# The high half of the weights stored as two areas of 16-column runs, read alternately by TensorE

## The reference: what is computed

```python
proj = h @ w_in[l]                       # 1024 x 7584, split into the branches
y_mla = mla_branch(...)                  # @ w_uq, @ w_ukv, @ w_o
y_conv = conv_branch(...)                # @ w_pw
y_ret = retention_branch(...)            # @ w_o
merged = gates[:, :, 0] * y_mla + gates[:, :, 1] * y_conv + gates[:, :, 2] * y_ret
x = x + rms_norm_2(merged @ w_out[l], ln_mix_post[l])
h = rms_norm_2(x, ln_ffn_pre[l])
f = (jax.nn.silu(h @ ffn_w_gate[l]) * (h @ ffn_w_up[l])) @ ffn_w_down[l]
x = x + rms_norm_2(f, ln_ffn_post[l])
```

## Time and profile before

| | |
|---|---|
| median of 3 runs | 1239.05 us |
| lowest, highest | 1238.3, 1243.12 us |
| span of the profiled execution, first to last instruction | 1235.8 us |
| what the median has beyond that span | 3.25 us |
| TensorE (PE) busy | 1205.2 us, 98% |
| VectorE (DVE) busy | 901.5 us, 73% |
| ScalarE (ACT) busy | 639.1 us, 52% |
| mean DMA rate | 175 GB/s |
| mean granted TensorE clock | 0.995 of 2.4 GHz |

### The profile page before, as it was taken

One profiled execution on the slowest core, in us unless ns is written; L12 is line 12 of the kernel. 1 busy time (PEld: TensorE's weight loads), 2 busy tenths in 40 slices (PEclk: granted clock), 3 DMA queues, 4 the chain that ended last, 5 costly groups with the idle time before them and its releaser, 6 DMA issues.

```text
span 1235.8 us, 19035 instructions
## 1 busy us (share of the span) xinstructions
PE 1205.2 (98%) x7597; PEld 1013.5 (82%) x7597; DVE 901.5 (73%) x1463; ACT 639.1 (52%) x1034; POOL 100.4 (8%) x163
## 2 busy tenths in 40 slices
PE   7999999999999999999999999999999999999998
PEld 3566778888988788787999987988788787999986
DVE  7998877757589998687666655589997687665553
ACT  4334565665556665545444544556575545444441
POOL 6300011101000200201000001000200201000000
PEclk9999999999999999999999999999999999999999
DMA  7635666434565555354766664565445355565552
GB/s 251 221 94 173 205 208 191 156 119 146 163 205 168 155 157 187 133 169 164 216 201 188 193 195 154 174 211 169 158 153 188 132 170 170 190 197 193 191 194 75
DMA packets 71958, 215.68 MB, mean 175 GB/s; under 512 B 16256, under 2 KB 19744, under 8 KB 71744
## 3 DMA queue, kind: packets, MB, share of 16 engines
q1 hardware_dynamic: 65008, 206.37, 52.0%
q0 software_dynamic: 2112, 6.97, 1.8%
q10 hardware_dynamic: 4752, 1.14, 0.4%
HBM read 208.95 MB, written 3.15 MB: 172 GB/s over the span
## 4 chain that ended last, share of the span: by engine, by line
PE 86%; DVE 8%; ACT 3%; issue 2%; POOL 1%; DMA 0%; DVEq 0%; POOLq 0%; ACTq 0%
PE acc L700 17%; PE acc L702 17%; PE acc L701 17%; PE acc L678 7%; PE acc L680 7%; PE acc L679 7%; PE acc L639 3%; PE mixed L1015 1%; DVE weights_lo L1776 1%; PE mixed L1112 1%; ACT junk L1279 1%; PE turned L755 1%; DVE h_T L1806 1%; PE mixed L999 1%; PE mixed L1008 1%
## 5 line engine op out<-in xcount | busy, mean ns | idle before, releaser
L1776 DVE TENSOR_TENSOR weights_lo<-weights_raw,weights_hi 128x1024 fp32r<-128x1024 f32 (+1 forms) x304 | 355.7, 1204 | 71.6 <-ACT weights_hi L1244 71.0
L1244 ACT ACTIVATE weights_hi<-weights_raw 128x1024 fp32r<-128x1024 f32 (+1 forms) x304 | 305.8, 1043 | 80.8 <-DMA weights_raw<-stream_dram 80.6
L700 PE MATMUL acc<-weights_hi,act_F_hi 128*128 128x512 f32 (+1 forms) x680 | 275.7, 406 | 5.6 <-DVE act_F_lo L1806 3.4
L702 PE MATMUL acc<-weights_hi,act_F_lo 128*128 128x512 f32 (+1 forms) x680 | 267.2, 393 | 0.0
L701 PE MATMUL acc<-weights_lo,act_F_hi 128*128 128x512 f32 (+1 forms) x680 | 265.4, 390 | 0.0
L678 PE MATMUL acc<-act_F_hi,weights_hi 128*128 128x256 f32 x624 | 173.6, 278 | 0.0
L679 PE MATMUL acc<-act_F_hi,weights_lo 128*128 128x256 f32 x624 | 172.5, 276 | 0.0
L680 PE MATMUL acc<-act_F_lo,weights_hi 128*128 128x256 f32 x624 | 172.4, 276 | 0.0
L700 PEld LDWEIGHTS acc<-weights_hi,act_F_hi 128*128 128x128 f32 x680 | 128.7, 189 | 34.2 <-DVE act_F_lo L1806 4.3
L702 PEld LDWEIGHTS acc<-weights_hi,act_F_lo 128*128 128x128 f32 x680 | 128.4, 189 | 28.4
L701 PEld LDWEIGHTS acc<-weights_lo,act_F_hi 128*128 128x128 f32 x680 | 128.7, 189 | 25.6
(11 more groups left out here) (339 smaller groups left out, 1923.6 us busy)
## 6 DMA issues: line engine op xcount, KB each, us to landing
weights_raw<-stream_dram SPq DMA_DIRECT2D x306, 512.0 KB, 3.7
weights_raw_more<-stream_dram SPq DMA_DIRECT2D x58, 512.0 KB, 4.3
gains<-rows_dram POOLq DMA_DIRECT2D x12, 512.0 KB, 4.8
weights_raw<-stream_dram SPq DMA_DIRECT2D x6, 416.0 KB, 3.1
weights_raw<-stream_dram SPq DMA_DIRECT2D x4, 384.0 KB, 3.5
x_T<-x_in_dram SPq DMA_DIRECT2D x4, 256.0 KB, 6.0
ssm_bc<-ssm_bc_dram SPq DMA_DIRECT2D x1, 1024.0 KB, 8.6
u_scratch<-u_T ACTq DMA_DIRECT2D x4, 256.0 KB, 5.5
```

The costliest lines, as they stand in the source:

```text
L700: pe.matmul(o, xh, wh, start=first and kk == 0, stop=False)
L702: i = pe.matmul(o, xl, wh, start=False, stop=last and kk == s["nk"] - 1)
L1244: act.activation(high(s, slice(0, n)), whole(s, slice(0, n)), ACT.Copy).then_inc(hi_made, 1)
L1776: dve.tensor_tensor(low(s, slice(0, n)), whole(s, slice(0, n)), high(s, slice(0, n)).bitcast(F32), ALU.subtract).then_inc(lo_made, 1)
```

## The change

In every slot that goes the rows-held way, the high half is stored in another order. The 1024 columns are taken as runs of 16 columns (64 bytes); the even runs go to the first half of the place, the odd runs to the second half, 2048 bytes further on. For the moving operand, TensorE gets an access pattern with three dimensions (16 pairs of runs, 2 areas, 16 columns), so that it takes a run from one area and a run from the other in turn. The columns reach the array in the old order, and the results are written to PSUM contiguously, as before. ScalarE writes the high half through the new pattern and VectorE reads it back through it; the raw weights and the low half keep their order. Slots that go the channels-held way are unchanged. No instruction is added, removed or moved on any engine, and no tile changes its address.

```diff
+LINE = 16
...
+        def channels_held(s):
+            name = slots[s]["chunk"]
+            return name in with_channels and not name.endswith(".ffn.0")
+
+        def halves_apart(s, x):
+            if channels_held(s):
+                return x
+            return x.rearrange("p (h i c) -> p i h c", h=2, c=LINE)
+
+        def lines_in_order(s, x):
+            if channels_held(s):
+                return x
+            return x.rearrange("p (i h c) -> p i h c", h=2, c=LINE)
+
+        def in_halves(s, kk):
+            n = slots[s]["nk"] * slots[s]["width"]
+            x = high(s, slice(0, n)).rearrange("p (h k i c) -> p k i h c", h=2, k=slots[s]["nk"], c=LINE)
+            return x[:, kk]
...
@@ tile_slot (rows held)
-                    wh, wl = (f(at, slice(kk * w, (kk + 1) * w)) for f in (high, low))
+                    wh, wl = in_halves(at, kk), low(at, slice(kk * w, (kk + 1) * w))
...
@@ make_hi, on ScalarE
-                act.activation(high(s, slice(0, n)), whole(s, slice(0, n)), ACT.Copy).then_inc(hi_made, 1)
+                act.activation(halves_apart(s, high(s, slice(0, n))), lines_in_order(s, whole(s, slice(0, n))), ACT.Copy).then_inc(hi_made, 1)
...
@@ make_lo, on VectorE
-                dve.tensor_tensor(low(s, slice(0, n)), whole(s, slice(0, n)), high(s, slice(0, n)).bitcast(F32),
-                                  ALU.subtract).then_inc(lo_made, 1)
+                dve.tensor_tensor(lines_in_order(s, low(s, slice(0, n))), lines_in_order(s, whole(s, slice(0, n))),
+                                  halves_apart(s, high(s, slice(0, n)).bitcast(F32)), ALU.subtract).then_inc(lo_made, 1)
```

## The result

The changed kernel takes **1257.47 us**, median of four runs (1255.34 to 1261.55), against 1238.67 us for the kernel before (four runs, 1235.68 to 1243.12). The ratio is 1.0158, 95% interval 1.0129 to 1.0187: **slower by 1.6%**, 18.8 us. The profiled execution took 1255.34 us with a span of 1253.5 us, 17.7 us more than the span before; the mean granted clock is 0.996 (0.995 before), so the clock plays no part.

The account below looks back on a forecast made before the run. TensorE was taken to set the pace, through the distance between matmuls. Span 1235.8 less 11.9 us from the high-half stream, other steps at nothing, gave 1223.9; plus 3.25 for the median, 1227 us, range 1213 to 1264.

Parts of the forecast that it names:

- The place: Effect expected in L700 and L702, 2030 matmuls streaming the high half; L701 and channels-held matmuls untouched.
- the two bounds: Rows-held high-half matmul: from 12.9 ns less (23.6 us gained) to 13.3 ns more (24.3 us lost).
- half of the excess: High-half stream: 16 of some 31 cycles beyond a clean stream saved per matmul, 6.5 ns, 11.9 us less.
- Rival 2: L700 and L702: each change of area costs one more TensorE cycle, 13.3 ns, 24.3 us slower, 1263; chance 0.28.
- Rival 1: Moving stream: fetch rate limits it whatever the order of 64-byte runs; no change, 1239 within 5; chance 0.30.
- Rival 3: High-half stream: all 12.9 ns come back, 23.6 us, 1215; upper part of the faster case, whose chance is 0.42.
- The term 1.83 us per ns: High-half matmuls: one nanosecond on each of 2030 is 2.03 us of streaming, 1.83 us of it on the chain.
- the share of 0.90: Rows-held lines: 630 us of their 697 us of streaming taken to lie on the chain that sets the end.
- The steps costed at nothing: ScalarE's write and VectorE's read in two areas: no cost taken; bad end 66 and 76 ns per slot, about 1 us.
- a faster TensorE that meets VectorE: Near 435 and 885 us VectorE has 2% left; a rows-held stream 2% shorter was said to just fit.
- The range: Whole kernel: from the clean stream, 1213, to one full cycle per run, 1264, leaving out only a larger loss.
- The chances: Whole kernel: faster 0.42, no change 0.30, slower 0.28.

Follow-up runs that it names:

- the fifth run: TensorE-only program, not the kernel: 512-column matmuls streaming every fifth 16-column piece, 320 bytes apart; 228.7 ns each, as contiguous.
- the runs of 64: The changed kernel with pieces of 64 columns in place of 16, slots of 416 columns contiguous; 1238.12 us, ratio 1.0002 to the kernel before.
- the areas at 2112 bytes: Kernel before, but TensorE alternates 16-column pieces from areas 2112 bytes apart, 128 bytes on in each, in 512-column slots; 1237.2 us, ratio 0.9998.
- the last row of the table: TensorE-only program: 16-column pieces from two areas 2048 bytes apart, 128 bytes on in each; 233.3 ns per matmul, one group.
- the stores alone: The changed kernel with TensorE reading the high half contiguously, ScalarE and VectorE keeping the two-area pattern; 1238.28 us, ratio 0.9999 to the kernel before.
- the first small program: No kernel: TensorE alone runs 24 matmuls for each of 28 access patterns; contiguous 228.7 ns, the change's pattern 240.0 ns.
- TensorE's pattern alone: The changed kernel with ScalarE's and VectorE's steps contiguous again, TensorE still reading two areas; 1261.91 us, ratio 1.0191 to the kernel before.
- runs of 32: The changed kernel with pieces of 32 columns in place of 16, slots not divisible by 64 contiguous; 1247.51 us, ratio 1.0081 to the kernel before.
- the last kernel: The kernel before with activation operands that only rows-held products read moved to the weights' address modulo 256 bytes; 1235.18 us, ratio 0.9981.

## Why the prediction was wrong

**What bounds the kernel** was read rightly: TensorE holds the chain before and after, nothing else got longer, and the whole difference is in the distance from one rows-held matmul to the next. **The place** was right too: the matmuls that stream the high half.

**The step that failed** is the choice of a value between the two bounds: "I take half of the excess as the gain: the two areas are 2048 bytes apart, so a pair of runs starts on equal low address bits, and wherever the cycle per run comes from changing to another part of the memory, it is then paid once in two runs." The observation about the address bits was the right one, and its sign was wrong. The change's pattern does not save half a cycle per run but costs 11.1 ns a matmul (228.9 to 240.0), 27 cycles, close to one more for each of the 32 runs. The excess of some 31 cycles in the contiguous stream has no part in it; it stayed in every pattern that was tried (the quickest had 226.7 ns), and a model of it that no row tested should not have been given the direction of the forecast.

**Rival 2** had the side and nearly the size: 13.3 ns and 24.3 us, against 11.1 ns and 18.8 us. Its mechanism was half right. "Each change of area costs one cycle" is refuted by the fifth run, by the runs of 64 and by the areas at 2112 bytes; its other reason, that "two areas with equal low address bits may hit the same part of the memory twice in a row", fits the change, though not the last row of the table. I held against it that jumps are free in the earlier trace rows. These rows are at half the column rate, where the contiguous stream, too, shows next to none of its excess. The eight runs of L895 lie 1024 bytes apart, 0 modulo 256, which at the full rate was among the dear steps (every fourth and eighth run, 240.0 ns), and still they cost nothing there. So that row could not have shown the loss, as the prediction itself says, and I still let it weigh.

**Rival 1** rested on the rule of the Trainium skill (Advanced Engine Details and Errata, section SBUF Cachelines) that full performance needs at least two accesses to a line of 16 bytes; the prediction concluded from it that the order of whole lines is free. The measurement decides against it for this stream: the same whole lines take 228.9 or 240.0 ns by the order of their addresses. **Rival 3**, the clean stream, was reached by no pattern: the quickest took 226.7 ns. The 215.8 ns that the Trainium skill (TensorE: Matmul & The Clock Gate, section Back-to-back issue gap) gives for 512 columns was not seen in this stream; the section gives it for a single isolated matmul, which the prediction did not say.

**The term 1.83 us per ns.** 705 or 715 against 686.7 is 23.3 ns more per three at the mean; times 1015 and the share of 0.90 that is 21.3 us, where the span grew 17.7. The share was therefore nearer 0.75. Added up over the whole trace, the distances behind L726 grew from 246.4 to 256.0 us, behind L728 from 248.8 to 254.0 and behind L727 from 234.3 to 237.8, together 18.3 us. Those under 260 ns alone grew by 24.3 us, and the longer ones, in which TensorE waits for something anyway, shrank by 6.0. The share of 0.90 left too little for these. Of the sum 3.5 us are L727's, for which I had forecast no change. Two slips in the working are too small to matter: eight more matmuls of L702, 416 columns on `weights_hi_more`, make 1021.5 out of 1015, and 3.4 ns a matmul is 0.25 of a cycle per run, not 0.2.

**The steps costed at nothing** held. ScalarE's and VectorE's steps stayed at 1055 and 1220 ns, the stores alone give a ratio of 0.9999, and TensorE's waits for low halves fell. The channels-held matmuls kept 113.3 ns in the changed kernel. The case of a faster TensorE that meets VectorE did not arise.

**The range** took its upper end from the full cycle per run, and the time lies inside. The chances did not show how little spoke for a gain: none of its rows held a stream of 512 columns at full rate that was quicker than 228.8 ns.

**Left open.** Why the residue modulo 256 bytes counts, that is what in the memory or on the way to the array has this period, no run shows. Nor is there a rule for alternating steps (246.7, 243.3, 233.3 ns), or for runs of 8 and 4 columns, which were dearer (243.2 and 249.2 ns). The cycle per 16 columns in the contiguous stream is untouched. Not tried: moving the weights for the channels-held way, for which there was no room in SBUF.

## What to carry to other kernels

Contiguity is not what kept the float32r stream of this kernel at its pace. Every pattern tried whose successive 64-byte pieces ascend by 64 modulo 256 bytes was as quick as the contiguous one, however far it jumped, and no other was. Before a layout is changed for TensorE's sake, time the pattern, at the tiles' own addresses, in a program of a few dozen matmuls: two groups of such a program had the answer here, 240.0 against 228.7 ns. Put each pattern in more than once, since one and the same stream was seen at 228.7 and at 233.4 ns (next section). And a row that shows something to be free at half rate is no evidence for the full rate.

## What the runs showed that was not expected

The relative position of stationary and moving operand modulo 256 bytes moves a 512-column matmul between 226.7 and 233.4 ns and a 256-column one, channels held, between 113.3 and 119.9, with the best place for one way being the worst for the other.

The same addresses can have two paces. L85 and L189 of the first small program read the same columns; L85 takes 228.7 ns a matmul and L189, which comes after other groups, (190.38 - 184.78)/24 = 233.3. The source describes L189's operand in more dimensions, but the trace records the same pattern for both, 512 successive columns, so to TensorE the two groups are alike but for the PSUM tile they write to. The granted clock is 1.00 in both, and no other engine works. In the kernel, whole feed-forward parts of channels-held products run at 353 or 354 ns per three in place of 340 in some kernels that did not touch them (338 places with TensorE's pattern alone and 319 with runs of 32, 26 in the kernel before, 20 in the changed one, 88 with runs of 64, 26 in the areas at 2112 bytes). Rows-held products do it too, at 700 ns per three in place of 687: the 64 places of the last kernel and, with the stores alone, six between 123 and 128 us. That is worth up to 4 us of a run, a fifth of the effect studied here, and it would be read as an effect of an edit by whoever compares only two times. What sets the pace off is not known.
